# Latent projections and their norms dealt out between the steps of local attention; the pattern count as a logarithm in the mask

## What is computed

```python
A_PATTERNS  # three (window, dilation) pairs
def mixer_ab(x, cos_a, sin_a, cos_b, sin_b, w_in, q_norm, w_q_up, kv_norm, w_kv_up, w_out):
    h = x @ w_in
    qa = apply_rope_2(h[..., :o1].reshape(shape_a), cos_a, sin_a, A_ROT)
    ka = apply_rope_2(h[..., o1:o2].reshape(shape_a), cos_a, sin_a, A_ROT)
    va = h[..., o2:o3].reshape(shape_a)
    out_a = dilated_mixture(qa, ka, va).astype(x.dtype)
    cq = rms_norm_2(h[..., o3:o4], q_norm, RMS_EPS)
    qb = (cq @ w_q_up).reshape(B, S, B_HEADS, B_NOPE + B_ROPE)
    q_pe = apply_rope_2(qb[..., B_NOPE:], cos_b, sin_b, B_ROPE)
    ckv = rms_norm_2(h[..., o4:o5], kv_norm, RMS_EPS)
    kv = (ckv @ w_kv_up).reshape(B, S, B_HEADS, B_NOPE + B_V)
    k_pe = apply_rope_2(h[..., o5:].reshape(B, S, 1, B_ROPE), cos_b, sin_b, B_ROPE)
    ...
    out_b = dense_attention(qb, kb, vb, (B_NOPE + B_ROPE) ** -0.5).astype(x.dtype)
    return jnp.concatenate([out_a, out_b], axis=-1) @ w_out
```

## Time and profile before

| | us |
|---|---|
| median of three runs | 1784.21 (1782.24 to 1786.38) |
| the profiled execution, its own time | 1783.27 |
| its span in the trace | 1781.5 |
| PE busy | 1652.4 (93%) |
| PE weight loads busy | 1407.7 (79%) |
| DVE busy | 1100.7 (62%) |
| ACT busy | 867.6 (49%) |
| share of PE in the chain that ended last | 78% |

### The profile page before, as it was taken

One profiled execution on the slowest core, in us unless ns is written; L12 is line 12 of the kernel. 1 busy time (PEld: TensorE's weight loads), 2 busy tenths in 40 slices (PEclk: granted clock), 3 DMA queues, 4 the chain that ended last, 5 costly groups with the idle time before them and its releaser, 6 DMA issues.

```text
span 1781.5 us, 23005 instructions
## 1 busy us (share of the span) xinstructions
PE 1652.4 (93%) x9768; PEld 1407.7 (79%) x9768; DVE 1100.7 (62%) x1332; ACT 867.6 (49%) x1004; POOL 8.6 (0%) x19
## 2 busy tenths in 40 slices
PE   6999999999999998989899888899999997999998
PEld 3687878699986776879798766699987884799986
DVE  5468463355576787886546657666556557665565
ACT  5455534635434776764343345454443436354443
POOL 0000000000000000000000000000000000000000
PEclk9899999899999999999999989999999998899999
DMA  6625312124645798986355222345544441445540
GB/s 226 220 95 190 108 70 73 47 95 145 237 167 188 286 327 305 357 316 251 132 194 175 88 81 85 119 167 193 202 172 146 150 164 37 142 167 199 179 166 24
DMA packets 132382, 297.70 MB, mean 167 GB/s; under 512 B 5207, under 2 KB 16776, under 8 KB 131320
## 3 DMA queue, kind: packets, MB, share of 16 engines
q1 hardware_dynamic: 130192, 287.93, 46.6%
q0 software_dynamic: 1184, 5.72, 1.0%
q10 hardware_dynamic: 904, 2.58, 0.5%
HBM read 295.17 MB, written 1.05 MB: 166 GB/s over the span
## 4 chain that ended last, share of the span: by engine, by line
PE 78%; DVE 12%; ACT 8%; issue 2%; DMA 1%; ACTq 0%; POOL 0%; DVEq 0%
PE bank L437 77%; DVE cut L1400 3%; ACT cut L2356 2%; PE bank L450 1%; ACT arena L2556 1%; DVE stat L1614 1%; ACT pairs L2362 1%; DVE XT L2224 1%; DVE pairs L2231 0%; DVE XT L2218 0%; DMA arena<-in_hy 0%; ACT arena L2565 0%; DMA raw<-in_w_in 0%; DVE stat L2204 0%; DVE arena L1421 0%
## 5 line engine op out<-in xcount | busy, mean ns | idle before, releaser
L1400 DVE TENSOR_TENSOR cut<-raw,cut 128x2048 fp32r<-128x2048 f32 (+1 forms) x268 | 606.1, 2275 | 401.1 <-ACT cut L2356 400.2
L437 PE MATMUL bank<-pairs,cut 128*128 128x256 f32 (+1 forms) x5480 | 690.2, 287 | 22.0 <-DVE cut L1400 10.7
L437 PEld LDWEIGHTS bank<-pairs,cut 128*128 128x128 f32 (+1 forms) x5480 | 678.4, 192 | 32.7 <-DVE cut L1400 18.0
L2356 ACT ACTIVATE cut<-raw 128x2048 fp32r<-128x2048 f32 (+1 forms) x268 | 506.2, 1900 | 357.8 <-PE bank L437 337.6
L437 PE MATMUL bank<-cut,pairs 128*128 128x512 f32 (+1 forms) x2460 | 592.3, 401 | 22.6 <-DVE pairs L1408 10.0
L437 PEld LDWEIGHTS bank<-cut,pairs 128*128 128x128 f32 x2460 | 465.0, 193 | 138.3 <-issue 19.4
L437 PE MATMUL bank<-arena 128*128 128x128 f32 (+10 forms) x748 | 184.4, 409 | 24.8 <-ACT arena L2395 7.6
L437 PEld LDWEIGHTS bank<-arena 128*128 128x128 f32 (+4 forms) x748 | 109.9, 194 | 79.6 <-issue 56.3
L2362 ACT ACTIVATE pairs<-arena 128x256 fp32r<-128x256 f32 (+1 forms) x81 | 37.6, 498 | 88.4 <-DVE arena L2268 51.8
L450 PEld LDWEIGHTS bank<-cst,arena 128*128 128x128 f32 x264 | 33.6, 154 | 43.4 <-DVE arena L1625 16.1
L450 PE MATMUL bank<-cst,arena 128*128 128x128 f32 x264 | 44.7, 303 | 21.5 <-DVE arena L1625 11.3
(11 more groups left out here) (291 smaller groups left out, 895.2 us busy)
## 6 DMA issues: line engine op xcount, KB each, us to landing
raw<-in_moe_w_gate SPq DMA_DIRECT2D x32, 1024.0 KB, 6.8
raw<-in_moe_w_up SPq DMA_DIRECT2D x32, 1024.0 KB, 5.5
raw<-in_moe_w_down SPq DMA_DIRECT2D x32, 1024.0 KB, 5.6
raw<-in_w_in SPq DMA_DIRECT2D x30, 1024.0 KB, 5.3
raw<-in_w_mod SPq DMA_DIRECT2D x24, 1024.0 KB, 5.3
raw<-in_ffn_w_gate SPq DMA_DIRECT2D x22, 1024.0 KB, 5.1
raw<-in_ffn_w_up SPq DMA_DIRECT2D x22, 1024.0 KB, 5.1
raw<-in_ffn_w_down SPq DMA_DIRECT2D x22, 1024.0 KB, 4.9
```

Of the source, the lines that this page charges most:

```text
L437: return pe.matmul(o, l, r, start=start, stop=stop, skip_group_check=True)
L1400: v.tensor_tensor(both[:, PIECE:PIECE + n], M.raw[K.place(i)[0]][:, 0:n], both[:, 0:n].bitcast(F32), ALU.subtract).then_inc(*up("lo_w", i))
L2356: a.activation(M.cut[K.slot(i)][:, 0:n], M.raw[K.place(i)[0]][:, 0:n], ACT.Copy).then_inc(*up("hi_w", i))
```

## The change

The mask tensor now holds log(count), with −1e30 where no pattern reaches, in 512 columns instead of 1024. The exponentials therefore come out multiplied by the count, ACT sums them while it computes them, and `counted` only divides. Between the local steps on PE now stand the latent projections (24 matmuls at a time), the sums of squares, the spreading of the roots and the rotation of kr. The norm is done over tokens as rows: squares summed by ten matmuls with one column, roots of 128×4 numbers, a diagonal 128×512 spread by one matmul with ones, and five multiplications. The four query tile pairs get a buffer each, and the rotations stand at other places among the kn matmuls.

```diff
-    neg = np.where(count > 0, 0.0, -1e30)
-    mask = np.concatenate([count.reshape(128, 512), neg.reshape(128, 512)], axis=1).astype(f)
+    mask = np.where(count > 0, np.log(np.maximum(count, 1.0)), -1e30).reshape(128, 512).astype(f)
...
+        self.RNl = self.RNb + e[0:2]
...
-    def group(name, m0, src, c0, nt, Xs, nk, free, width=128, banks=Q, hook=None):
+    def group(name, m0, src, c0, nt, Xs, nk, free, width=128, banks=Q, hook=None, each=None):
...
+                if each and 2 * i + 2 < len(units):
+                    each()
...
+            if each:
+                each()
...
-    for i in range(8 + 3):
+    units = iter(range(8 + 3))
+
+    def local_step():
+
+        i = next(units)
...
-            weighed_half("b", i - 3, 64 * (i - 3), ((i - 3) % 4,))
-
-
-    project("lc", W, 1536, 5, (X,), 8, lambda m: ("LC", m))
+            weighed_half("b", i - 3, 64 * (i - 3), ((i - 3) % 2,))
+
+
+    def latent_sums():
+
+        o = claim(("nss", "latent"), ("nn", "latent"), (2,))
+        for c, (name, X2, nk) in enumerate((("lq", M.CSQ, 3), ("lk", M.CSK, 2))):
+            P.wait_ge(*at("sq", name, 0))
+            for i in range(2):
+                last = chain(o[:, 2 * c + i:2 * c + i + 1], [(X2[:, k, 128 * i:128 * i + 128], C("ones")[:, 0:1])
+                                                             for k in range(nk)])
+        last.then_inc(*up("nss", "latent"))
+
+    local_step()
+    group("lc", 0, W, 1536, 4, (X,), 8, lambda m: ("LC", m), banks=(2, 3), each=local_step)
+    group("lc", 4, W, 2048, 1, (X,), 8, lambda m: ("LC", m), banks=(2,), each=local_step)
     h = take(W, 0, 8, 1952, 256)
-    o = claim(("kr",), ("CR",), Q)
+    o = claim(("kr",), ("CR",), (3,))
...
-    plain_sums("lq", 3)
-    plain_sums("lk", 2)
+    local_step()
+    latent_sums()
+    local_step()
+    norm_spread("latent", M.RRl, 512)
+    local_step()
     P.wait_ge(*at("CRz"))
-    rotate(("kr", 0), ("CR",), C("Rb")[0:96, 0:96], M.CR[0:96, :], 96, A4)
+    rotate(("kr", 0), ("CR",), C("Rb")[0:96, 0:96], M.CR[0:96, :], 96, (3,))
+    local_step()
+    local_step()
...
-        if h0 == 2:
-            lq_turn(4)
+        if h0 < 4:
+            lq_turn(2 * h0)
...
-        v.tensor_tensor(E, E, M.AM[:, 0:512], ALU.mult).then_inc(*up("v"))
-        w(*at("v"))
-        v.tensor_reduce(M.cols(("b", u, "l"), 2), E.rearrange("p (g n) -> p g n", g=2), AX.X, ALU.add).then_inc(*up("v"))
-        w(*at("v"))
         divided("b", u, E, 2)
...
+        if i == 7:
+            norm_spread("latent", LR, M.RRl)
...
-    plain_norm("lq", M.CQ, 3, "ab_q_norm_2", ("CQS", M.CQS))
-    plain_norm("lk", M.CK, 2, "ab_kv_norm_2", ("CKS", M.CKS))
...
-            weights("b", i, M.Eb[i % 3], M.Eb[i % 3], 2, 1.0, False)
+            weights("b", i, M.Eb[i % 3], M.Eb[i % 3], 2, 1.0)
...
+        if 3 <= i < 6:
+            latent(2 * i - 6)
+        if i == 5:
+            for key, x, x2, m in (("lq", M.CQ, M.CSQ, 2), ("lk", M.CK, M.CSK, 4)):
+                w(*at("LC", m))
+                a.activation(x2, x, ACT.Square).then_inc(*up("sq", key, 0))
```

More of the change, by code:

```diff
@@ L409, in lay_out @@
         self.CR, self.CRR = e[3][:, 0:256], e[3][:, 256:512]
-        self.CQS, self.CKS = pair(b + 6144, 3, "CQS"), pair(b + 8192, 2, "CKS")
+        parts = lambda o, k: self.pairs[:, o:o + 256 * k].rearrange("p (k t) -> p k t", k=k)
+        self.CQS = Op(parts(b + 3072, 3), parts(b + 1024, 3), None)
+        self.CKS = Op(parts(b + 4608, 2), parts(b + 5632, 2), None)
+        self.RNl = self.RNb + e[0:2]
         self.A0 = f(b, 1024, 2)
@@ L2129, in masked @@
             w(*at("pt", "b", u - 3))
-        v.scalar_tensor_tensor(out=E, in0=M.bank[K.bank("s", "b", u)][:, :], scalar=0.125, in1=M.AM[:, 512:1024],
+        v.scalar_tensor_tensor(out=E, in0=M.bank[K.bank("s", "b", u)][:, :], scalar=0.125, in1=M.AM,
                                op0=ALU.mult, op1=ALU.add).then_inc(*up("ms", u))
@@ L2148, in vector_program @@
             counted(i - 1)
+        if i == 7:
+            norm_spread("latent", LR, M.RRl)
+    sums = M.bank[2]
+    w(*at("nbc", "latent"))
+    for key, x, nk, gname, c0 in (("lq", M.CQ, 3, "ab_q_norm_2", 0), ("lk", M.CK, 2, "ab_kv_norm_2", 256)):
+        for k in range(nk):
+            v.scalar_tensor_tensor(out=x[:, k, :], in0=x[:, k, :], scalar=M.vcol(gname, k), in1=sums[:, c0:c0 + 256],
+                                   op0=ALU.mult, op1=ALU.mult).then_inc(*(up("nn", "latent") if c0 and k == nk - 1 else
+                                                                          up("pn", key, k)))
+    w(*at("CR"))
+    w(*at("rots", 1))
+    v.tensor_tensor(M.CRR[64:96, :].unsqueeze(1), M.CR[64:96, :].unsqueeze(1), wide(M.cosB[64:96, :], 1),
+                    ALU.mult).then_inc(*up("v"))
+    for name, x, nk, dst in (("CQS", M.CQ, 3, M.CQS), ("CKS", M.CK, 2, M.CKS)):
+        for j in range((nk + 1) // 2):
+            c = slice(2 * j, min(2 * j + 2, nk))
+            cut_lo(name, j, dst.lo[:, c, :], x[:, c, :], dst.hi[:, c, :])
+    turn_sin(("kr", 0), M.CRR[64:96, :].unsqueeze(1), M.sinB[64:96, :], M.RCb[0], 1, 64, 96)
     for j in range(2):
@@ L2810, in half_out, with latent, latent_roots @@
         a.activation(M.MX[p, tile, :], M.bank[K.bank("y", name, u)][p, 0:256], ACT.Copy).then_inc(*up("YA", name, u))
+    CQK = [M.CQ[:, 0, :], M.CQ[:, 1, :], M.CQ[:, 2, :], M.CK[:, 0, :], M.CK[:, 1, :]]
+    def latent(m0):
+        w(*at("pj", "lc", m0))
+        for j in range(min(2, 5 - m0)):
+            a.activation(CQK[m0 + j], M.bank[K.bank("pj", "lc", m0)][:, j * 256:j * 256 + 256],
+                         ACT.Copy).then_inc(*(up("LC", m0) if j or m0 == 4 else up("a")))
+    def latent_roots():
+        w(*at("nss", "latent"))
+        LR = M.cols("latent_roots", 4)
+        for c, d in enumerate((384, 256)):
+            x = slice(2 * c, 2 * c + 2)
+            a.activation(LR[:, x], M.bank[2][:, x], ACT.Sqrt, scale=1.0 / d,
+                         bias=C("eps")[:, 0:1]).then_inc(*(up("nro", "latent") if c else up("a")))
     for i in range(8 + 3):
+        if i == 7:
+            latent_roots()
         if i < 8:
-            weights("b", i, M.Eb[i % 3], M.Eb[i % 3], 2, 1.0, False)
+            weights("b", i, M.Eb[i % 3], M.Eb[i % 3], 2, 1.0)
         if 2 <= i < 8 + 2:
@@ L2830, in scalar_program @@
         cut_hi("XSm0", j, M.XS.hi[:, 2 * j:2 * j + 2, :], M.MX[:, 2 * j:2 * j + 2, :])
[L2831 to L2848 removed]
+    for m in (0, 2, 4, 6):
+        copied("lq", m, M.RNl[m // 2], ("bk", m // 2 % 2 * 2), 96)
     for h0 in range(0, 8, 2):
```

75 lines of the change are left out of this document (21 added, 54 removed).

## The result

| | before | after |
|---|---|---|
| median, us | 1782.24 (1778.64 to 1786.38) | 1766.71 (1761.93 to 1774.76) |
| profiled execution, us | 1783.27 | 1768.38 |
| span in the trace, us | 1781.5 | 1766.6 |

What follows compares the result with a forecast made beforehand. DVE was taken to bound local attention, with waits in the norm after it. Gains of 21.0 us up to lq and 0.7 behind it, 21.7 in all, gave 1762.5 us, range 1757.5 to 1770.

Steps and rivals of the forecast that it cites:

- What bounds the kernel: Local attention to latent attention: DVE fills the 3.68 us local steps; PE then waits 2.60 and 5.25 us in the norm.
- rival 1: Tail from 36.3 us: the clock falls to 1.2 GHz, adding 1.5 to 7 us; 1765.5 us, chance 0.27.
- The first part: First scores to lq: PE never waits in the dense steps, done at 31.4; lq at 45.3 instead of 66.3, 21.0 us.
- The cover for DVE and ACT: Dense local steps: PE's 5.4 us a step covers DVE's 4.6 and ACT's at worst 5.2, costing nothing.
- Rival 3: Dense steps: ACT is late and each of six chunk steps loses 2 us; 1774.5 us, chance 0.07.
- The tail of the norm: Step 6's end to lq, 13.9 us: sums 2.4, PE waits from 36.3 to 38.4 ahead of the spread.
- Rival 2: ACT: each function switch costs 1.4 us beyond its load, 2.8 in all; 1765.3 us, chance 0.05.
- The second part: lq to latent scores: 22.3 us against 23.0, a gain of 0.7 us.
- The two rotation waits: Between lq and latent scores: PE's last rotation and kn's third pair wait for rotation banks 0 and 2, 1.5 us.
- The sum: Whole stretch: 21.0 + 0.7 = 21.7 us, latent scores at 67.6 instead of 89.3.

Runs made afterwards that it cites:

- e2: The kernel before with only the mask and `counted` changed (logarithm of the count in the mask); median 1775.35 us, ratio 0.9952.
- e3: The changed kernel with the old mask, count multiplied in and summed on DVE; median 1767.78 us, ratio 0.9904.
- e1: The changed kernel with the copy of the second pair of latent tiles moved ahead of head 4's exponentials on ACT; median 1762.80 us, ratio 0.9867.
- e5: e1 plus a 256-column filler matmul behind each one-column sum but the last, written into idle bank 7; median 1762.06 us, ratio 0.9879.
- e4: The changed kernel with a 256-column filler matmul behind each one-column sum but the last, in the sums' own bank; median 1763.77 us, ratio 0.9891.
- e8: e5 plus value projections in banks 6 and 7 and the latents' high parts cut ahead of output 6 on ACT; median 1758.76 us, ratio 0.9861.
- e7: e1 with the old mask, count multiplied in and summed on DVE; one execution of 1773.25 us.

## Why the prediction was right and wrong

**What bounds the kernel: right.** DVE filled the local steps and the norm's two waits followed; e2 takes the first away, e3 the second. Direction and kind of gain were as forecast; its size was 15.5 us by the medians and 13.2 in the stretch instead of 21.7. The time, 1766.7, lies in the range, and that is in part luck: the range reached so far up only for the fall of the clock (rival 1). The clock fell, but cost far less than the 7 us allowed, and the bank's wait, which no rival named, took up the rest.

**The first part: one sentence failed.** "The new waits that the chunks bring (bank 2 or 3 free once ACT has copied) are a step old as well." They are not. The chunk's results were complete in time, but I asked how old the data were and not where their copy stands on ACT. It stands behind the exponentials of the very step that PE has just begun, so the chain is scores, mask, exponentials, copy of the transposes, output, copy. This is 5.4 us (1031.35 to 1036.75), and PE has only 2.65 of other work in it (scores, transposes, weighed values). Left is a wait of 2.9. It costs 1.45 us more because the clock falls and the chunk behind it takes 4.51 for 3.06. e1 shows both at once. The rest of the 5.4 us, about 1.1, is sizes: a chunk has a pitch of 3.06, not 2.9, and a step takes 2.65, not 2.5. The row that I divided, 14.54 for 119, was of one unbroken run.

**The cover for DVE and ACT: right.** PE waits for DVE nowhere in the dense steps of after: its only wait there is the one for ACT's copy. e3, where DVE has 1.44 us more a step, shows the edge of this cover: two waits of 0.57 and 0.40. Rival 3, which would have had each step lose 2 us, did not occur as a series; its one instance is the copy above.

**The tail of the norm: the wait was right in place, its cause of loss was not.** I forecast 2.1 us ahead of the spread. It is 0.39 in after, and 1.74 at full clock in e5, where the fillers keep PE busy for about 1 us longer. Without them it would be some 2.2 (PE there 1.05 us earlier, the spread 0.6 earlier), an estimate. By it the tail would take some 13.6 us at full clock, close to my 13.9. The step took 16.43 because rival 1 occurred: the clock fell, 2.2 us net by e4, and some 2.8 if the fillers' own 0.6 is taken off. I had put the fall behind the wait; it came ahead of it, at the end of the one-column sums. The sums themselves were right (2.58 for 2.4). What I had as the end of the chain, the roots on ACT, was not last in after: they were done at 1054.81, and DVE took them at 1056.54, behind the mask of head 7 and the division of head 6. I had counted the diagonal right behind the roots.

**Rival 2, the function switch: fell.** ACT's timeline after, the second place in this trace where it can be seen:

```profile
1053.11 1.28 ACT L2844 ACT_TABLE_LOAD   x1
1054.40 0.41 ACT L2844 ACTIVATE stat<-bank,cst 128x2 f32<-128x2 f32 x2
1054.83 1.28 ACT L2575 ACT_TABLE_LOAD   x1
1056.13 0.51 ACT L2575 ACTIVATE arena<-arena,stat 128x256 f32<-128x256 f32 x1
```

Load, roots, load and exponentials follow each other within 0.02 us. The load agrees with the 1283 ns of the Trainium skill (ScalarE: Activation LUTs, What ACT_TABLE_LOAD costs); its drain of some 1380 ns is not in this trace either. By it, as an estimate, these four instructions would take 2.8 us longer than measured.

**The second part: right within 0.6 us.** 22.86 for 22.3. The two rotation waits that I named are there, 0.72 and 0.22. What I left out is the wait of 0.78 ahead of the latent scores, whose bank the values still held; e8 removes it.

**The sum.** Of the 8.5 us that the latent scores came too late, 5.4 lie ahead of the end of step 6 (4.4 of them the bank's wait with its clock), 2.5 in the tail (the clock) and 0.6 behind lq. The total gained 15.5 where the stretch gave 13.2; the rest lies in parts that the change doesn't touch.

**Mask plus dealing.** The prediction added nothing twice, but it also never said what each edit brings alone. Its picture, PE never waiting, is one in which the mask matters only through cover. e2, e3 and e7 give it numbers: 9.6 alone, and on top of the dealing 0.3 or 3.2. In both of these DVE's two instructions cost some 2.2 us, 0.8 in the dense steps and 1.44 in the tail, and the place where the clock fell did the rest.

What stays open: what sets the moment at which the clock falls, from 0.6 us ahead of the sums' end to 1.9 behind it over four kernels with one trace each; what the logarithm is worth at a steady clock; and how much of the last 1.74 us at the spread can go. To take the roots on DVE ahead of the division of head 6 was not tried; by e5's rows it could give up to 0.6 us, an estimate.

## What to carry to other kernels

When work is dealt out between the steps of a pipeline, check for each bank or buffer it reuses not only when its data are complete but where the instruction that frees it stands in its engine's list, and what that list waits for ahead of it: here a copy of 0.66 us held PE for 2.9, and moving it gave 4.2 us where the whole change had given 13.2. Two edits that remove the same wait do not add, so measure each alone before crediting one. Read a change between two markers of the trace when identical code ahead of it varies by several us from one execution to the next. Even between the markers, look where the clock fell before you price an edit: the same two instructions showed as 0.3 us in one pair of kernels and as 3.2 in another.

## What the runs showed of the hardware

- The granted clock fell to the lower level at twenty records of one-column matmuls (2.4 to 2.6 us) in which PE showed as busy, in each of the four kernels with these sums alone. It fell 0.5 and 0.6 us ahead of their end in after and e7, 0.3 behind it in e1 and 1.9 behind it in e3, and stayed low for 10 us in the first two and 7 in the others. With nine matmuls of 256 columns between them it stayed at 1.00 in each of the three kernels that had them (e4, e5, e8). A busy PE in the record is thus no sign that its clock will hold.
- A wait of 2.9 us behind 21 us of dense work was followed by 4 us at 0.57, with the chunk at 4.51 instead of 3.1; e4 repeats it (2.89, then 4.61), and e3 (2.46, then 4.61). With a wait of 0.17 the chunk ran at full clock, and a wait of 1.74 in e5 left the clock at 1.00 too.
- A half clock costs little where the engine would else have waited for another. In after (against e4) 10 us at the lower level cost 0.1 us up to the spread and 2.1 behind it; in e1 (against e5) 7 us cost 1.05 behind it, and up to it e1 was 0.43 faster, without the fillers.
